# Retention's query, key and gate products for all heads first, 15 of 16 block pairs in the seven-product form

## The reference

```
def retention_mixer(a_ctx, a_lat, w_in, decay_param, w_out, want_ctx):
    log_gamma = -jnp.exp(decay_param.astype(jnp.float32))
    def project(a, rope):
        q, k, v, g = jnp.split(a @ w_in, [hk, 2 * hk, 2 * hk + hv], axis=-1)
        if rope is not None:
            q, k = apply_rope(q, *rope), apply_rope(k, *rope)
    ...
    o_ctx, o_lat = bidirectional_scan(ctx_terms, lat_terms)
    def readout(o, g):
        y = rms_norm_2(o).transpose(0, 2, 1, 3).reshape(B, n, hv).astype(g.dtype)
        return (jax.nn.silu(g) * y) @ w_out
```

## Time and profile before

| | |
|---|---|
| median of 3 runs | 2790.18 us (2788.88 to 2790.49) |
| span of the profiled execution | 2789.8 us |
| mean granted TensorE clock | 0.999 |
| PE busy | 2760.5 us, 99% |
| VectorE (DVE) busy | 1891.0 us, 68% |
| ScalarE (ACT) busy | 1236.5 us, 44% |
| GpSimd (POOL) busy | 405.2 us, 15% |
| DMA | 267.91 MB, mean 96 GB/s |

### The profile page before, as it was taken

How to read it: one execution, slowest core, us unless ns; L and a number is a source line. 1 busy time by engine, 2 the same in 40 slices (tenths; PEclk the granted TensorE clock), 3 DMA queues, 4 the chain that set the end, 5 groups by cost and what they waited for, 6 DMA issues and landing times.

```text
span 2789.8 us, 42554 instructions
## 1 busy us (share of the span) xinstructions
PE 2760.5 (99%) x16554; PEld 2456.6 (88%) x16554; DVE 1891.0 (68%) x3427; ACT 1236.5 (44%) x2249; POOL 405.2 (15%) x222
## 2 busy tenths in 40 slices
PE   8999999999999999999999999999999999999998
PEld 8888896988888888888888999999997787989898
DVE  7788788868896653444435896566685636777686
ACT  5332358642233552332314654344355546545354
POOL 2233300023323011011011000000001323000000
PEclk9999999999999999999999999999999999999999
DMA  6565512236554211111011112222223121222322
GB/s 206 186 187 190 165 64 83 84 102 222 189 188 137 77 53 61 38 61 61 31 61 53 40 57 79 63 67 72 72 76 102 50 76 52 76 84 91 106 92 84
DMA packets 86025, 267.91 MB, mean 96 GB/s; under 512 B 9153, under 2 KB 18753, under 8 KB 85569
## 3 DMA queue, kind: packets, MB, share of 16 engines
q1 hardware_dynamic: 85824, 265.20, 29.6%
HBM read 261.49 MB, written 2.10 MB: 94 GB/s over the span
## 4 chain that ended last, share of the span: by engine, by line
PE 94%; DVE 3%; ACT 1%; issue 1%; DMA 1%; SPq 0%; DVEq 0%; ACTq 0%
PE ps L2113 30%; PE ps L2114 29%; PE ps L2115 29%; PE ps L2392 1%; PE ps L2376 1%; PE ps L2365 1%; DMA t_x<-in_x 0%; DVE t_wlo L2810 0%; PE ps L2257 0%; PE ps L2249 0%; PE ps L2308 0%; PE ps L2265 0%; PE ps L2298 0%; DVE t_m L3128 0%; DVE t_m L2927 0%
## 5 line engine op out<-in xcount | busy, mean ns | idle before, releaser
L2113 PE MATMUL ps<-t_h,t_whi 128*128 128x512 f32 (+2 forms) x2152 | 726.7, 338 | 7.7 <-DVE t_tmp L2840 3.2
L2114 PE MATMUL ps<-t_h,t_wlo 128*128 128x512 f32 (+2 forms) x2152 | 721.2, 335 | 0.0
L2115 PE MATMUL ps<-t_h,t_whi 128*128 128x512 f32 (+2 forms) x2152 | 721.1, 335 | 0.0
L2435 ACT CAST t_whi<-t_raw 128x1024 fp32r<-128x1024 f32 (+3 forms) x449 | 367.8, 828 | 570.5 <-PE ps L2115 372.6
L2113 PEld LDWEIGHTS ps<-t_h,t_whi 128*128 128x128 f32 x2152 | 407.9, 190 | 51.0 <-issue 10.4
L2114 PEld LDWEIGHTS ps<-t_h,t_wlo 128*128 128x128 f32 x2152 | 408.0, 190 | 36.5 <-issue 1.2
L2115 PEld LDWEIGHTS ps<-t_h,t_whi 128*128 128x128 f32 x2152 | 407.9, 190 | 35.6
L2113 PE MATMUL ps<-t_hid,t_whi 128*128 128x256 f32 (+2 forms) x1320 | 428.2, 324 | 1.8 <-DVE t_hid L3107 1.7
L2114 PE MATMUL ps<-t_hid,t_wlo 128*128 128x256 f32 (+2 forms) x1320 | 425.7, 322 | 0.0
L2115 PE MATMUL ps<-t_hid,t_whi 128*128 128x256 f32 (+2 forms) x1320 | 425.1, 322 | 0.0
L2810 DVE TENSOR_TENSOR t_wlo<-t_raw,t_whi 128x512 fp32r<-128x512 f32 (+3 forms) x360 | 321.7, 903 | 111.8 <-ACT t_whi L2435 108.7
(11 more groups left out here) (357 smaller groups left out, 4836.5 us busy)
## 6 DMA issues: line engine op xcount, KB each, us to landing
t_raw<-in_gu SPq DMA_DIRECT2D x174, 512.0 KB, 3.4
t_raw<-in_ada SPq DMA_DIRECT2D x96, 512.0 KB, 3.8
t_raw<-in_dn SPq DMA_DIRECT2D x52, 512.0 KB, 4.2
t_raw<-in_dn SPq DMA_DIRECT2D x24, 384.0 KB, 3.4
t_raw<-in_ret_v SPq DMA_DIRECT2D x16, 512.0 KB, 3.3
t_raw<-in_ret_qk SPq DMA_DIRECT2D x16, 512.0 KB, 3.3
t_raw<-in_ret_g SPq DMA_DIRECT2D x16, 512.0 KB, 3.4
t_raw<-in_ret_o SPq DMA_DIRECT2D x16, 512.0 KB, 3.8
```

The costliest lines, as they stand in the source:

```text
L2113: e.matmul(out, whi, xlo, start=first, stop=False, skip_group_check=shared)
L2114: e.matmul(out, wlo, xhi, start=False, stop=False, skip_group_check=shared)
L2115: return e.matmul(out, whi, xhi, start=False, stop=last, skip_group_check=shared)
L2435: e.copy(m.block(0, it.slot, n), m.raw(it)).then_inc(*S["hi"].of(j))
```

## The change

The query, key and gate products of all heads move ahead of the first `attend`. Before them stand `v_rows(0)`, the sums T1 to T4 of the tokens (`token_sums`, `last_sums`: with three tokens' parts of 384 columns) and the decay tables of all four heads. Pair 0 of head 1's gates is computed as before (`plain_gates(1, 0)`); the other 15 pairs are `seven_pair`s, with 84 matmuls of 384 columns each. Values of head 0, decay tables, queries and keys of heads 1 to 3, and all gates are stored to device memory by DMAs that ScalarE issues (`v_store`, `dec_store`, `qk_store`, `g_store`) and loaded by SyncE's queue when used. Each decay table is computed in the same place of `t_m`, so `decays` of a head waits for the landing of the store before it (`d_ds`). After `attend(3)`, ret_o follows with no products between.

```diff
+        def decays(h, after):
+            put("ret_decay", h=h, after=after, slot=[e for k in range(4) for e in slots.get(("b", k), [])])
             free([("b", k) for k in range(4)], ("ret_gs", h))
-            ov["p"][0] = ov["p"][0] + [("ret_act", ("ll", h))]
-            ov["p"][1] = ov["p"][1] + [("ret_act", ("ll", h))]
+            put("dec_store", h=h)
+            return [("d_ds", h)]
...
+        def gate_store(h, c, half, t0, n, off, keys_, name):
+            put("g_store", h=h, c=c, half=half, t0=t0, n=n, off=off, name=name)
+            free(keys_, (name, (h, c, half)))
+            stores[h].append((name, (h, c, half)))
...
+        def plain_gates(h, i):
+            def post(g, c):
+                off, after, keys_ = tmp("a", g.n)
+                half = 2 + g.t0 // 512
+                put("g_plain", h=h, c=c, half=half, g=g.id, bank=g.bank, t0=g.t0, n=g.n, off=off, after=after)
+                gate_store(h, c, half, g.t0, g.n, off, keys_, f"d_gp{off // 256}")
+            columns([(("ret_g", h * 4 + c), (SLOT,), DC, ("h", 4), [(0, "drain_act", lambda g, c=c: post(g, c))]) for c in (2 * i, 2 * i + 1)], SEG2)
+
...
+        def seven_pair(what, h, i):
+            key, n = ("ret", what, h, i), 384
+            ops = pair(*((("ret_qk", i * 8 + h * 2 + k) if what == "qk" else ("ret_g", h * 4 + 2 * i + k)) for k in range(2)))
+            banks = {"P1": bank(), "P2": bank(), "P5": bank()}
+            banks.update(P6=banks["P1"], P7=banks["P1"], P4=banks["P1"], P3=banks["P5"])
...
+
+            def product(name, q, x, before):
...
+                ids[name] = g.id
+                tick(4 * (n + 32) / 800)
+                over(j, "ps", g.id)
+
+            def snap(name):
...
+            def add(name, copied, off, g):
+                put("seven_add", key=(*key, name), off=off, g=ids[g], bank=banks[g], n=n, out=None, after=[], snap=(*key, copied))
+
+            def gate(name, k, half, off, keys_):
+                put("g_silu", key=(*key, name), h=h, c=2 * i + k, half=half, off=off, n=n)
+                gate_store(h, 2 * i + k, half, half * n, n, off, keys_, f"d_gs{off // 384}")
...
+            product("P1", "A11", "B11", seat(banks["P1"], "drain_dve" if what == "qk" else "drain_act", (*key, "C21")))
+            s1, keys1 = snap("P1")
+            product("P5", "S1", "T1", seat(banks["P5"], "drain_dve", (*key, "C12")))
+            s5, keys5 = snap("P5")
+            product("P6", "S2", "T2", [("snap", (*key, "P1"))])
+            s2, keys2 = snap("P6")
+            offs, at = {(0, 0): s1, (0, 1): s2, (1, 1): s5}, (0, 1, 2, 3)
+            product("P3", "S4", "B22", [("snap", (*key, "P5"))])
+            add("C12", "P6", s2, "P3")
+            if what == "g":
+                gate("C12", 0, 1, s2, keys2)
+            product("P7", "S3", "T3", [("snap", (*key, "P6"))])
+            add("C22", "P5", s5, "P7")
+            if what == "g":
+                gate("C22", 1, 1, s5, keys5)
+            else:
+                put("rope_late", key=key, h=h, w=i, offs=offs, sides=at, after=sides[0])
+                sides[0] = [("rq", (h, i, 1, 1))]
+                for k in range(2):
+                    split(k, 1)
+                    free((keys2, keys5)[k], ("rq_lo", (h, i, k, 1)))
+            product("P2", "A12", "B21", seat(banks["P2"], "drain_dve", (*key, "C11")))
...
+                put("rope_first", key=key, h=h, w=i, offs=offs, sides=at, after=sides[1])
+            product("P4", "A22", "T4", [("drain_dve", (*key, "C22"))])
...
+                gate_store(h, 2 * i + 1, 0, 0, n, off, keys_, f"d_gs{off // 384}")
+            else:
+                put("rope_second", key=key, h=h, w=i, offs=offs, sides=at, g=ids["P4"], bank=banks["P4"], after=sides[2] + sides[3])
...
+                if h:
+                    put("qk_store", h=h, w=i)
+                    ov["qk"][i] = [(f"d_qs{i}", h)]
+                    staged[i] = (f"d_qs{i}", h)
+            return ids
...
-            from_bank(4)
-            return columns([(("ret_g", h * 4 + c), (SLOT,), DC, ("h", 4), [(0, "drain_act", lambda g, c=c: post(g, c))]) for c in range(4)],
-                           SEG2[::-1] if h == n_head - 1 else SEG2)
-
+        def gated_values(h, t0, n):
+            for c in range(4):
+                put("ret_y", h=h, c=c, t0=t0, n=n)
+                put("ret_split", h=h, c=c, t0=t0, n=n)
+
...
-        decays(0)
+        put("v_store")
+        pro = state["misc_free"] + [("ps", ("root", "nf2", s)) for s in range(2)] + [("ada", (1, 47, who)) for who in range(2)]
+        put("ret_setup", after=pro + state["hid_free"])
+        token_sums("ret", 4, 384, pro)
+        last_sums("ret", 4, 384, pro)
+        late = pro
         for h in range(n_head):
-            queries_keys(h)
+            late = decays(h, late)
+        put("rope_load", after=[("ret_act", ("ll", n_head - 1))])
+        sides[:] = [late] * 4
+        plain_gates(1, 0)
+        wide_slots(384)
+        ov["qk"] = [[("d_vs0", 0)], [("d_vs0", 0)]]
+        state["quad"] = [("gate_pool", ("f2", "rs", s)) for s in range(2)]
+        gate_pairs = [(1, 1), (2, 0), (2, 1), (3, 0), (3, 1), (0, 0), (0, 1)]
+        pairs = [(h, w) for h in (1, 2, 3, 0) for w in range(2)]
+        for k, (h, w) in enumerate(pairs):
+            seven_pair("qk", h, w)
+            if k != 3:
+                last = seven_pair("g", *gate_pairs[k - (k > 3)])
+        back_to_slots(384)
+        last_h = [("ps", last["P4"])]
+        rope_done = sides[0] + sides[1] + sides[2] + sides[3]
+        put("dec_load", h=0, after=rope_done + [("d_ds", n_head - 1)])
+        put("v_load", after=[("ps", last["P6"])])
+        put("g_load", h=0, after=last_h + stores[0])
+        ov.update(oc=last_h, p=[rope_done, rope_done, last_h], v=[])
...
+        for h in range(n_head):
             attend(h)
             ov["v"] = [("ret_ps", ("v", h, 0, 5, 3))]
-            ov["st"] = [("drain_dve", ("ret_p", h, 0, 5))]
-            state["h_free"] = [gates(h)]
-            ov["oc"] = [("ret_lo", (h, t0, 3)) for t0 in (512, 0)]
-            ov["p"][2] = ov["p"][2] + ov["oc"]
                 v_rows(h + 1)
-                decays(h + 1)
+                state["h_free"] = [("ps", max(it.id for it in items if it.kind == "group"))]
...
+    def dec_store(it):
+        w.wait_ge("ret_ll", it.h)
+        w.wait_ge("ret_gs", it.h)
+        e.dma_start(dram["s_dec"][it.h], m.at(RTAB, 1536)).then_inc(*S["d_ds"].of(it.h))
...
+    def v_store(it):
+        for tt in range(6):
+            w.wait_ge("drain_act", (("ret_v", 0), tt))
+            w.wait_ge("drain_dve", (("ret_v", 0), tt))
+        for part in range(2):
+            e.dma_start(dram["s_v"][part], m.HID[:, part * 4096:part * 4096 + 3072].bitcast(F32)).then_inc(*S["d_vs0"].of(("part", part), 0))
...
+    def g_store(it):
+        w.wait_ge("drain_act", ("g", it.h, it.c, it.half))
+        e.dma_start(dram["s_g"][it.h, :, it.c, it.t0:it.t0 + it.n], m.tmp(it.off, it.n)).then_inc(*S[it.name].of((it.h, it.c, it.half)))
```

More of the change, by code:

```diff
@@ L242, in note @@
             takes, lasts = 480, 3300
+        if name == "dma_start" and self.engine != "sync":
+            takes, lasts = 100, 3400
         it, piece = self.here
@@ L687, in rows, with rows_by_group @@
             pass
-    def rows_by_group(srcs, ver, after, key, dest, order=(4, 5, 0, 1, 2, 3), pairs=False, banks=(), early=0, low_dest=None):
+    def rows_by_group(srcs, ver, after, key, dest, order=(4, 5, 0, 1, 2, 3), pairs=False, banks=(), early=0, low_dest=None, aside=False):
         held = [block(s, (SLOT,)) for s in srcs]
@@ L1003, in token_sums, with last_sums @@
                              for e in slots.get((ab, k), [])]
-    def last_sums(f, ver, n, last):
-        read = [last]
+    def last_sums(f, ver, n, read):
         for c in range(DC // 2):
-            put("t4_full", f=f, ver=ver, c=c, n=n)
+            put("t4_full", f=f, ver=ver, c=c, n=n, after=read)
             put("t4_hi", f=f, c=c, n=n, after=read)
@@ L1748, in schedule @@
             it["taken"] = [(name, it.old + QUADS.index("S4")) for name in ("hi", "lo_dve")] if it.old is not None else []
+            it["taken"] = it.taken + it.over
         if it.kind == "prep":
@@ L1940, in ret_v, with v_row @@
         return self.MW[:, o:o + P]
+    def v_row(self, it, part):
+        o = (it.dst, it.low)[part]
+        return self.HID[:, o:o + 512] if it.aside else self.MW[:, o:o + 512]
     def ret_raw(self, at, n):
@@ new lines, in v_store, with rope_hi @@
+    def v_store(it):
+        for tt in range(6):
+            w.wait_ge("drain_act", (("ret_v", 0), tt))
+            w.wait_ge("drain_dve", (("ret_v", 0), tt))
+        for part in range(2):
+            e.dma_start(dram["s_v"][part], m.HID[:, part * 4096:part * 4096 + 3072].bitcast(F32)).then_inc(*S["d_vs0"].of(("part", part), 0))
+    def rope_hi(it):
+        w.wait_ge("rq", (it.h, it.w, it.k, it.half))
+        wait_all(it.after)
```

(22 more changed lines are left out.)

346 lines of the change are left out of this document (199 added, 147 removed).

## The result

The changed kernel takes 2969.09 us (median of 4 runs, 2966.57 to 2970.24) against 2790.34 us: 1.064 times the time before, with a 95% interval of 1.0625 to 1.0655. I had forecast slower, but 2829 with a range to 2853. The excess is 178.8 us where I had worked out 40.

What follows compares the result with a forecast made beforehand. TensorE was taken to bound the kernel, with 643.94 of 644.00 us busy in retention. Waits of 71.5 us less 31.2 saved gave +40.3, 2830.5, lowered for overlap to 2829 us; range 2797 to 2853.

Steps and rivals of the forecast that it cites:

- The saving: Retention's 15 seven-product pairs: 14.56 us each instead of 16.64, so 2.08 a pair and 31.2 us less in all.
- P5's wait: First seven-product pair: P5 needs a PSUM bank that ScalarE empties late, at the first gate read; stall 17.4 us.
- P6's: First seven-product pair: P6 waits for the second gate block and copies behind store landings; stall 6 to 8.5, taken as 7.
- P7's: First seven-product pair: P7 waits for P6's copy, behind all four serial decay tables on ScalarE; stall 32.6 us.
- The steady pairs: Later pairs in retention: VectorE 88% busy over two pairs, giving waits of 0 to 6 us, taken as 3.
- the term of 3.5: Rest of the first pair and the next: copies stand behind the store of the first queries on ScalarE; 0 to 6 us.
- The loads: Load of v (3 MB), issued at the last P6, lands about when needed: 1 us, bounds 0 and 5.
- The end: After head 3: only ret_o of the context rows covers the latent rows' norm; stall 7 us, 6 to 10.
- Everything else TensorE does is moved, not changed: TensorE's work outside the seven-product pairs: only its place in the order changes, so no saving or cost of its own.
- the sum of +40: Whole kernel: waits of 71.5 us less 31.2 saved, +40.3 on the span of 2789.8.
- The one on VectorE as the bound: Rival for all pairs: each two pairs take a tenth longer, 22 us, 2851; chance 0.13 for above 2848.
- The clock: Half speed for one product behind each of four long waits: 8 us, 2837; chance 0.3, counted in the forecast's case.

Runs made afterwards that it cites:

- e7: Changed kernel, planner untouched, with the load of the distances listed ahead of head 0's v rows instead of behind them: 2787.10 us, 0.9990 of before.
- e8: e7 with head 0's table load ahead of the last gate pair, v's load behind that pair's P6, gate pair (3, 1) in the old form: 2779.28 us.
- e1: Changed kernel with the planner's due-time walk keeping listing order for SyncE and TensorE alone: 2808.11 us, 1.0062 of before.
- e5: e1 with tables made in two places, gate pair (1, 1) ahead of the first query pair, head 0's table load ahead of the last gate pair: 2789.32 us.
- e6: e5 with gate pair (3, 1) computed in the old form after head 3's values: 2787.26 us, 0.9992 of before.

## Why the prediction was wrong

- **The saving**: 2.08 us a pair, 31.2 in all, held. In e7 ten of the 13 pairs from the second to the 14th take 14.56 us from the start of one to the next, within 0.02, and none over 15.9. e8 has 14 such pairs, a saving of 29.1 us, and ends 12 below before. TensorE's waits in retention, 11 us summed in e8 against none over 0.15 us in before, are the larger part of the difference.
- **P5's wait, 17.4**: measured 18.2. **P6's, 7**: 4.0, and the lower clock's part on top. **P7's, 32.6**: 29.1; the table store landed in 3.2 us and not 4.4, which is a period of 9.1 us a head. From P1 of the first pair to P1 of the second it is 71.65 us, so 57.1 are lost where these three terms make 57.0. That it comes so close is luck: the waits for P6 and P7 are 3.0 and 3.5 us shorter than forecast, and the lower clock fills in. The steps were right for the order in which they were read, and that order was itself a symptom: in e1 the first wait is gone, in e7 the largest too.
- **The steady pairs, 3**: mis-sized. The stage up to the scores takes 344.5 us; its products are 144 x 0.227 + 16.64 + 15 x 14.56 = 267.7, so 76.8 are lost, where my terms for it make 63.5. The 14 pairs behind the first lose 18.7 of them, where I had 6.5 with the term of 3.5: small waits for `t_wlo` and for copies (13.0 us in sum), and the clock. In e1 the same pairs lose 2.0, so these too came from the lost due times.
- **The loads, 1**: 8.4 us. I took v for the late one; it was head 0's table, whose load stands in SyncE's queue behind weight loads that wait for a place: it was issued at 1264.5, 3 us after the first scores' products had started, and landed 7.4 us later. I had counted the transfers and not the queue they are listed in. v would have been the next to wait for (4.9 us in e5).
- **The end, 7**: in e1, with sound due times, the stage from the last value product to ffn3 takes 124.6 us, before without its gate blocks 150.1 - 33.3 = 116.8: 7.8 us, and the filler of e6 took 4.4 of them (125.6 us in e5, 137.8 - 16.6 in e6). My own terms, 19.4 - 11.5, make 7.9 and not the 7 that went into the sum. In the changed kernel the same stage loses 48 us.
- **The step that failed** is the sentence "Everything else TensorE does is moved, not changed", and the sum that ended at ffn3. The planner places VectorE's, ScalarE's and GpSimd's orders and TensorE's small products anew for every program, and here it did so with the due times lost. Measured against the sum of +40, the stages up to ffn3 lose 105, 65 more, and the stages behind it 72, where I had put nothing; with sound due times the whole kernel is 19 above before (e1). In the norm behind head 3 TensorE now stands at products that VectorE can't have ready. TensorE's timeline:

```profile
1609.57 0.70 PE L2347 MATMUL ps<-t_m,t_con 128*128 128x256 f32 x2 [2.85 <-DVE t_m L3099]
1615.64 1.22 PE L2384 MATMUL ps<-t_con,t_m 128*128 128x128 f32 x4 [5.37 <-DVE t_m L3099]
1618.01 1.22 PE L2392 MATMUL ps<-t_tmp,t_con 128*128 128x128 f32 x4 [1.14 <-DVE t_tmp L3159]
1626.81 0.58 PE L2248 MATMUL ps<-t_mw,t_whi 128*128 128x256 f32 x1 [7.58 <-DVE t_mw L3591]
```

and VectorE's, which is working on head 3's last rows and two norms at once:

```profile
1607.91 1.08 DVE L3093 TENSOR_TENSOR t_m<-t_m,t_x 128x256 f32<-128x256 f32 x3
1609.10 0.42 DVE L3099 TENSOR_TENSOR t_m<-t_m 128x256 f32<-128x256 f32 x1
...
1611.97 1.09 DVE L3093 TENSOR_TENSOR t_m<-t_m,t_tmp 128x256 f32<-128x256 f32 x3
1612.98 1.08 DVE L3174 TENSOR_TENSOR t_x<-t_x,ps 128x256 f32<-128x256 f32 x3
1613.97 1.09 DVE L3093 TENSOR_TENSOR t_m<-t_m,t_tmp 128x256 f32<-128x256 f32 x3
1615.17 0.42 DVE L3099 TENSOR_TENSOR t_m<-t_m 128x256 f32<-128x256 f32 x1
...
1626.07 2.49 DVE L3591 TENSOR_TENSOR t_mw<-t_m,t_mw 128x512 fp32r<-128x512 f32 x4
```

The sign of it stood in the order quoted with the change: L2347, L2384 and L2392 are there in adjoining rows behind the 96 context products. In the kernel before 78 ret_o matmuls lie between the first and the second of them and 21 (18 and 3) between the second and the third, time for VectorE's part of each. I read those rows for the cover of head 3's norm and not for the norm behind it.
- **The rivals**: none of mine named the planner. The one on VectorE as the bound would have explained waits in every pair, and e1 excludes it as the main cause: same operations, 161 us less.
- **The clock**: the lower level came, which before's own rows didn't show. P5 after its wait of 18.2 us, and the windows of 970 to 1030:

```profile
987.66 0.66 PE L2248 MATMUL ps<-t_mw,t_whi 128*128 128x384 f32 x1 [18.18 <-ACT t_tmp L2852]
...
991.00 0.52 PE L2249 MATMUL ps<-t_mw,t_wlo 128*128 128x384 f32 x1
991.32 0.52 PE L2250 MATMUL ps<-t_mw,t_whi 128*128 128x384 f32 x1
```

```profile
970.00:1000.00 30.00, 8.34 (x25) 7.90 (x26) 16.65 (x40) 19.70 (x44) 0.00 (x0) 0.54 0.46 175
1000.00:1030.00 30.00, 2.11 (x13) 1.79 (x11) 12.07 (x18) 10.11 (x13) 0.00 (x0) 0.61 0.22 84
```

Matmuls of 384 columns start 0.32 us apart, against 0.173; the granted clock is 0.54 and 0.61, the 1.2 GHz level for most of it, behind a TensorE that was idle for 18 us. By the rule of the Trainium skill that I had weighed ("TensorE: Matmul & The Clock Gate", Part 1), the trace agrees. A product at that level costs 12 x 0.147 = 1.8 us more. The granted clock is at the lower level for 175 us of the changed kernel's span, most of it while TensorE stands still (6.9 us in before, all at the very end). The 347 matmuls that start in those stretches take 33 to 45 us more from start to start than the usual distance of their size, the lower number for the matmuls of 256 columns and more alone. So some 33 to 45 of the 179 us are the clock's, where I had worked out 8. It follows the waits: in e1, where most of these are gone, the lower level lasts 48 us.

What stays open: how the 132 us of lost due times split between VectorE's order and the places of TensorE's small products, which e1 puts right together; and from which of the two the changed kernel's small waits in the pairs come.

## What to carry to other kernels

Where a planner or a pool decides orders, a change to one stage can undo the order of stages it doesn't touch. Compare the program before and after far behind the edit: if the small products stand elsewhere or an engine's order differs where no work differs, explain that before any sum is made. And for each transfer that is moved, ask what is listed ahead of it in its queue: moving the distances' load in the list made 21 us (e1 against e7), two thirds of the 31.2 that the arithmetic saved.
